# X loaded by column quarters and transposed before it is normalised, with the norm applied at the projections' outputs

## The chip, the cores and the metric

The kernel runs on one core of one Trainium2 chip. The metric is the time of one execution on the device, in microseconds (us). The kernel before takes 2932.31 us, the median of three runs (2931.34 to 2933.71).

## The reference, cut to what matters

The input is x, 256 tokens by 2048 columns, float32. Two attention layers come first (the loop over DEPTH below), then a third mixed layer, an expert layer and a final norm. The change touches the front of each of the two attention layers: the norm and the two kinds of projection by w_in.

```
def _rms_norm(x, g):
    xf = x.astype(jnp.float32)
    y = xf * lax.rsqrt(jnp.mean(xf * xf, axis=-1, keepdims=True) + NORM_EPS)
    return (y * g.astype(jnp.float32)).astype(x.dtype)

def _layer(x, g_pre, g_post, w_in, ...):
    h = _rms_norm(x, g_pre)
    proj = jnp.einsum('bsd,de->bse', h, w_in)
    (a_q, a_k, a_v, a_g, b_cq, b_ckv, b_kr, b_g, c_q, c_k, c_v, c_g) = jnp.split(proj, ...)
    ...                      # three attentions, each times silu of its gate
    y = jnp.einsum('bse,ed->bsd', jnp.concatenate([o_a, o_b, o_c], axis=-1), w_out)
    return x + _rms_norm(y, g_post)
```

The scale 1/rms is one number for each token. It can be multiplied in before the product with w_in or behind it.

## The kernel before

All matrix products are made from split operands: a float32 matrix is cut into a high part and a low part, and three products (high by high, low by high, high by low) are summed. The weights come from HBM as a stream of units of 128x2048 numbers (1 MB) into `ring`, which has four slots (R = 4); SyncE (SP) issues their loads, the next one of a slot when the slot's low part has been taken (`lo_done`). For each unit ScalarE (ACT) copies the high part to `wh` (`high`, `next_high`), VectorE (DVE) subtracts to get the low part `wl` (`low`, `next_low`), and TensorE (PE) then makes its products and adds one to `unit_done`. Four units are a group.

A layer has TM_G = 6 groups of products with tokens as rows (`rows_group`, result in PSUM, then to `PT`), FM_G = 6 groups with features as rows (`up`, result to `PF`), one group for latents, the attention in 8 rounds, and 4 groups of the output projection (`PLACE`). In this text unit n of a layer is the n-th of the first stage, counted from 0: PE makes 16 products with `wh` in it (L532) and then 8 with `wl`.

Ahead of the first group the operand is made. GpSimd (POOL) gives `rstd2`, the 1/rms of each token, from square sums that ACT makes in the first layer (`square_sums`); for the second layer POOL works it out from sums of the output projection. DVE multiplies X by it, block by block of 512 columns (`normed`, to `Xn`, `xn_done`); PE transposes `Xn` in four parts of 8 transposes (`transposed`, L601, `ht_full`); ACT takes from PSUM the high part `hh` of each chunk, with the gain `gcol` as its scale (`nh_done`), and DVE the low part `hl` (`nl_done`). Unit s of group 0 needs part s of both (`norm_part`). In the second layer X itself is first completed by `x_block`, which needs `yr` of POOL.

Beside this runs a second stream: 192 tiles of the matrix `in_ada`, loaded by POOL's queue into the two slots of `aring` and reduced by DVE (`modulation`, L1941), which belongs to the third layer and is spread over the whole program. DVE's loop over the units of the first stage is `if j > 1: next_low(...)` and then `modulation(l_ada, j)`, so the first two tiles stand ahead of the low part of unit 3, and everything on DVE runs in the order in which it is written. POOL issues the first tile behind `rstd_of(0, sq_done, prs_done)`. No scheduler moves anything; the order on each engine is that of the code, save that the compiler places the loads of ACT's function tables (ACT_TABLE_LOAD).

`keep_awake(n, bank)` makes n products of the identity with itself, of which nobody reads the result. Before, 40 of them stand at the end of each layer.

Of the kernel before, what the change touches and what calls it, by code (L numbers as in the profile page):

```python
# [23 lines left out]
P = 128  # L24
# [4 lines left out]
ALU = mybir.AluOpType  # L29
# [21 lines left out]
R = 4  # L51
# [29 lines left out]
ADA_TM, ADA_FM, ADA_ATT, ADA_WO = 22, 18, 2, 16  # L81
# [86 lines left out]
FM_MODS = [()] * 11 + [(0,), (1, 2), (3,), (4, 5), (6,), (7, 8), (9,), (10, 11), (12,), (13, 14), (15,), (16,), (17,)]  # L168
# [31 lines left out]
def block(nc, stream, ada, cond, small, const1, const2, decays, keys, nbr_bias, g_post, g_final, x, out):  # L200
# [8 lines left out]
    with ctx:  # L209
# [69 lines left out]
        krot = area(0, 2, T, 64)  # L279

# [101 lines left out]
        x_load = [sem(f"x_load{j}") for j in range(3)]  # L382
# [19 lines left out]
        yrs_done = sem("yrs_done")  # L402
        pe_passed, pool_passed, dve_passed = sem("pe_passed"), sem("pool_passed"), sem("dve_passed")
# [45 lines left out]
        def _(sp):  # L449
            sp.dma_start(ring[:, 0, :], stream[0]).then_inc(w_ready[0], 16)  # L450
            sp.dma_start(SM[:, :], small).then_inc(small_ready, 16)
            sp.dma_start(X[:, 0, :], x[0, 0:P, :]).then_inc(x_load[0], 16)
            for half in range(2):
                cols = slice(half * (DM // 2), (half + 1) * (DM // 2))
                sp.dma_start(X[:, 1, cols], x[0, P:2 * P, cols]).then_inc(x_load[1 + half], 16)
            sp.dma_start(crow, cond.rearrange("p (a b) -> p a b", a=2)).then_inc(cond_ready, 16)
            for s in range(1, R):
# [38 lines left out]
        def _(pe):  # L496
# [85 lines left out]
            def prenorm(i, banks):  # L582

                for b in range(8):
                    if b % 2 == 0:
                        pe.wait_ge(xn_done, i * 8 + (b + 2))
# [7 lines left out]
            def transposed(i, part, banks=T_BANKS):  # L594

                pe.wait_ge(xn_done, i * 8 + 2 * (part + 1))
                for b in (2 * part, 2 * part + 1):
                    for kk in range(2):
                        k = 2 * b + kk
                        for t in range(T):  # L600
                            last = pe.transpose(ps[:, banks[b], kk * SEQ + t * P:kk * SEQ + (t + 1) * P],  # L601
                                                Xn[:, t, k * P:(k + 1) * P], ident)
                    last.then_inc(ht_full, 1)

            pe.wait_ge(small_ready, 16)
            with pe.Fori(0, LAYERS) as l:
                for part in range(3):
                    transposed(l, part)
                for i in range(TM_G - 2):
                    rows_group(l * LAYER_G + i, l * TM_N + i, i % 2, layer=None if i else l, rest=() if i else ((l, 3),))  # L610
                for p, cols in ((0, 512), (1, TM_END)):
# [2466 lines left out]
```

## Time and profile before

| what | value |
|---|---|
| median of 3 runs | 2932.31 us (2931.34 to 2933.71) |
| the profiled execution | 2940.65 us, span 2939.0 us |
| PE busy | 2896.1 us, 99% of the span |
| PE weight load busy | 2480.1 us, 84% |
| DVE busy | 2127.9 us, 72% |
| ACT busy | 1309.7 us, 45% |
| POOL busy | 331.1 us, 11% |
| mean granted clock of PE | 0.995 |
| DMA | 620.62 MB, mean 211 GB/s |

The span is the time from the first to the last instruction of the profiled execution. A busy PE is not a PE at its peak, since the ends of pipelined matmuls are modelled; what the table says is that PE hardly ever waits. What can be gained or lost by an edit away from PE is thus in the few places where PE does wait.

### The profile page before, as it was taken

How to read it: one execution, taken by the hardware profiler on the slowest of the kernel's cores; microseconds unless marked ns; L12 is line 12 of the kernel's file. 1: busy time of each engine (PE TensorE's matmuls, PEld its weight loads, DVE VectorE, ACT ScalarE, POOL GpSimd, SP SyncE). 2: the span in 40 equal slices, each digit the busy share in tenths (PEclk: the TensorE clock that was granted, in tenths of full speed). 3: DMA queues.
4: the chain of work that ended last, by engine and by line, in shares of the span. 5: the costliest groups of instructions: out<-in, count | busy, mean ns of one | idle time of the engine just before them, and what ended most of it. 6: DMA issues, size and time to landing. Idle time of an engine off the chain costs nothing.

```text
span 2939.0 us, 43097 instructions
## 1 busy us (share of the span) xinstructions
PE 2896.1 (99%) x15984; PEld 2480.1 (84%) x15984; DVE 2127.9 (72%) x2852; ACT 1309.7 (45%) x1660; POOL 331.1 (11%) x359
## 2 busy tenths in 40 slices
PE   7999999999999999999999999999999999999998
PEld 6888788888788898988888888888888888887886
DVE  5687777687776857777489688447874488888745
ACT  5343444443544334754355444444443444444433
POOL 1011020011021101020088300000000000000001
PEclk9999999999999999999999999999999999999999
DMA  8867477766567867266545544555455554454553
GB/s 318 297 220 280 171 261 261 276 249 243 196 233 268 305 252 265 92 216 228 186 172 186 186 179 178 187 199 186 173 183 186 195 188 175 171 186 173 189 196 143
DMA packets 99614, 620.62 MB, mean 211 GB/s; under 512 B 11056, under 2 KB 11184, under 8 KB 37040
## 3 DMA queue, kind: packets, MB, share of 16 engines
q1 hardware_dynamic: 70560, 509.88, 48.3%
q0 software_dynamic: 28944, 109.26, 10.5%
q8 instruction: 71, 1.16, 0.2%
q14 instruction: 39, 0.32, 0.0%
HBM read 616.99 MB, written 2.10 MB: 211 GB/s over the span
## 4 chain that ended last, share of the span: by engine, by line
PE 90%; DVE 4%; DMA 3%; issue 1%; ACT 1%; POOL 1%; DVEq 0%; POOLq 0%; SPq 0%; ACTq 0%
PE ps L568 29%; PE ps L1015 17%; PE ps L532 15%; PE ps L578 15%; PE ps L1091 5%; DMA aring<-in_ada 2%; PE ps L977 1%; PE ps L741 1%; DVE wl L1925 1%; DVE aring L1941 1%; ACT BIG L1180 1%; PE ps L780 0%; PE ps L856 0%; PE ps L662 0%; PE ps L716 0%
## 5 line engine op out<-in xcount | busy, mean ns | idle before, releaser
L1180 ACT ACTIVATE wh<-ring 128x2048 fp32r<-128x2048 f32 (+1 forms) x498 | 894.6, 1802 | 1320.0 <-PE ps L578 668.3
L1925 DVE TENSOR_TENSOR wl<-ring,wh 128x2048 fp32r<-128x2048 f32 (+1 forms) x433 | 985.9, 2277 | 570.2 <-ACT wh L1180 308.6
L568 PE MATMUL ps<-hhl,wh 128*128 128x512 f32 x3680 | 889.9, 394 | 0.2 <-ACT wh L1180 0.2
L568 PEld LDWEIGHTS ps<-hhl,wh 128*128 128x128 f32 x3680 | 677.6, 189 | 132.9 <-issue 0.9
L578 PEld LDWEIGHTS ps<-hhl,wl 128*128 128x128 f32 x3680 | 471.7, 191 | 18.7 <-DVE wl L1925 0.8
L578 PE MATMUL ps<-hhl,wl 128*128 128x256 f32 x3680 | 477.1, 283 | 0.4 <-DVE wl L1925 0.4
L532 PE MATMUL ps<-wh,hhl 128*128 128x512 f32 (+1 forms) x1728 | 403.9, 386 | 2.2 <-issue 1.8
L532 PEld LDWEIGHTS ps<-wh,hhl 128*128 128x128 f32 x1728 | 320.2, 189 | 66.1 <-issue 3.7
L1941 DVE SCALAR_TENSOR_TENSOR aring<-aring,BIG 128x1024 f32<-128x1024 f32 x192 | 233.0, 1220 | 52.8 <-DMA aring<-in_ada 51.0
L532 PE MATMUL ps<-wl,hhl 128*128 128x512 f32 (+1 forms) x864 | 209.0, 384 | 1.4 <-DVE wl L1925 1.4
L1706 POOL DMA_DIRECT2D aring<-in_ada x192 | 102.3, 533 | 856.7 <-DVE aring L1941 839.0
L1015 PE MATMUL ps<-wh,stage_h 128*128 128x512 f32 x736 | 196.9, 389 | 0.0
L1015 PE MATMUL ps<-wl,stage_h 128*128 128x512 f32 x736 | 196.7, 389 | 0.0
L1015 PE MATMUL ps<-wh,stage_l 128*128 128x512 f32 x736 | 196.7, 389 | 0.0
L532 PEld LDWEIGHTS ps<-wl,hhl 128*128 128x128 f32 x864 | 159.6, 188 | 32.9 <-DVE wl L1925 2.0
L1822 POOL TENSOR_TENSOR wl<-ring,wh 128x1024 fp32r<-128x1024 f32 x62 | 152.0, 2480 | 125.9 <-ACT wh L1180 125.9
L1015 PEld LDWEIGHTS ps<-wh,stage_l 128*128 128x128 f32 x736 | 138.2, 188 | 28.7
L1015 PEld LDWEIGHTS ps<-wl,stage_h 128*128 128x128 f32 x736 | 138.2, 188 | 28.7
L1180 ACT ACTIVATE BIG<-ps 128x256 f32<-128x256 f32 (+5 forms) x171 | 100.0, 591 | 139.7 <-PE ps L532 84.9
L1015 PEld LDWEIGHTS ps<-wh,stage_h 128*128 128x128 f32 x736 | 137.9, 188 | 28.8 <-DVE stage_l L2540 0.4
L1827 POOL TENSOR_TENSOR X<-X,act 128x512 f32<-128x512 f32 x4 | 5.1, 1300 | 1275.3 <-DVE act L2886 1275.3
L1091 PE MATMUL ps<-wh,pairs 128*128 128x512 f32 x480 | 136.1, 395 | 1.7 <-DVE pairs L2755 1.7
(311 smaller groups left out, 2502.8 us busy)
## 6 DMA issues: line engine op xcount, KB each, us to landing
ring<-in_stream SPq DMA_DIRECT2D x480, 1024.0 KB, 4.8
aring<-in_ada POOLq DMA_DIRECT2D x192, 512.0 KB, 5.0
BIG<-in_nbr_bias POOLq DMA_DIRECT2D x2, 1024.0 KB, 6.2
BIG<-in_g_post POOLq DMA_DIRECT2D x2, 1024.0 KB, 5.6
out<-X SPq DMA_DIRECT2D x4, 512.0 KB, 2.7
BIG<-in_decays POOLq DMA_DIRECT2D x2, 768.0 KB, 5.9
X<-in_x SPq DMA_DIRECT2D x1, 1024.0 KB, 7.1
X<-in_x SPq DMA_DIRECT2D x2, 512.0 KB, 8.9
```

Source lines behind the costliest of these rows:

```text
L532: last = mm(ps[:, 2 * pair + t, 0:cols], lhs[:, k, tok], rhs[:, s % 2, w], start=s == 0 and kk == 0 and j == 0, stop=s == R - 1 and kk == ...
L568: mm(ps[:, 4 + c, :], wh[:, c % 2, k * P:(k + 1) * P], hhl[:, k, :, :].rearrange("p a b -> p (a b)"), start=(k == 0), stop=False, skip_gro ...
L578: last = mm(ps[:, 4 + c, 0:SEQ], wl[:, c % 2, k * P:(k + 1) * P], hh[:, k, :], start=False, stop=(k == KD - 1), skip_group_check=True)
L741: last = mm(ps[:, 6 + buf, hh2 * SEQ:(hh2 + 1) * SEQ], v, probT[buf][:, hh2, kt, :], start=(kt == 0), stop=(kt == 1))
L977: last = mm(ps[:, bank + j // 4, at:at + GATE_PARTS * PART], hot1[:, b, j, :], hot2[:, b, :, j, :], start=True, stop=True)
L1015: last = mm(ps[:, 4 * t + d, :], lhs[:, c % 2, tok], rhs[:, c % 2, d * 512:(d + 1) * 512], start=first and j == 0, stop=last_unit and j == ...
L1091: last = mm(ps[:, 4 * t + 2 * p + d, :], pairs[c % 2][:, part, i2, tok], rhs[:, c % 2, at:at + 512], start=first and i2 == 0 and j == 0, s ...
L1180: return nc.scalar.activation(o, i, func, **kw)
L1706: pool.dma_start(aring[:, h, :], ada[first + i, h]).then_inc(a_ready[h], 16)
L1822: pl.tensor_tensor(wl[:, c % 2, cols], ring[:, c, cols], wh[:, c % 2, cols].bitcast(F32), ALU.subtract).then_inc(lo_done if half else lo_h ...
L1925: return tt(blocks(wl[:, c % 2, :], cols), blocks(ring[:, c, :], cols), blocks(wh[:, c % 2, :].bitcast(F32), cols), ALU.subtract)
L1941: stt(w, w, 1.0, crow[:, h, :], ALU.mult, ALU.mult, accum_out=mod_parts[:, bass.ds(first * 2 + j, 1)]).then_inc(a_used, 1)
```

## The change

- SP loads the small constants first, then in turn a quarter of X's columns (all 256 tokens by 512 columns, `x_load[0..3]`) and a weight unit; `cond` comes after unit 2.
- PE begins with 16 identity products. It transposes X itself, not `Xn`, each part as its quarter has landed; parts 0 and 1 stand ahead of unit 0, parts 2 and 3 between units 0 and 1. In the second layer each part waits for its `x_block` alone. The loop over the two layers is written out on PE. The 40 identity products behind layer 0 become 20; behind layer 1 they stay 40.
- `normed` goes from both layers. The scale is put in later: ACT's copies of the first stage's groups become two each, one for each token tile, with scale `rstd2` (`rooted_out`); for the second stage PE makes a row of the scales in PSUM by two products (`root_row`), DVE copies it to `rrow`, and POOL multiplies each of the 24 chunks of `PF` by it (`fm_scaled`). ACT's Silu of a gate chunk now waits for this product. The table `FM_MODS` puts 16 instead of 18 tiles of `in_ada` into the second stage, and the first has 24 instead of 22.
- In the first layer ACT makes the square sums behind the high part of unit 3, no longer at the start, and the high and low parts of unit 0 come after the first two chunks of the operand.

```
             sp.dma_start(SM[:, :], small).then_inc(small_ready, 16)
+            for s in range(R):
+                cols = slice(s * 512, (s + 1) * 512)
+                sp.dma_start(X[:, :, cols], x[0, :, cols].rearrange("(t p) c -> p t c", t=T)).then_inc(x_load[s], 16)
                 sp.dma_start(ring[:, s, :], stream[s]).then_inc(w_ready[s], 16)
+                if s == 2:
+                    sp.dma_start(crow, cond.rearrange("p (a b) -> p a b", a=2)).then_inc(cond_ready, 16)
...
+            def root_row(l):
+
+                pe.wait_ge(prs_done, l + 1)
+                for t in range(T):
+                    last = mm(ps[:, 7, t * P:(t + 1) * P], rstd2[:, t:t + 1].to_broadcast([P, P]), ident, start=True, stop=True)
+                last.then_inc(rrow_full, 1)
+
             pe.wait_ge(small_ready, 16)
-            with pe.Fori(0, LAYERS) as l:
-                for part in range(3):
+            keep_awake(16, 7)
+            for l in range(LAYERS):
+                for part in range(2):
                     transposed(l, part)
                 for i in range(TM_G - 2):
-                    rows_group(l * LAYER_G + i, l * TM_N + i, i % 2, layer=None if i else l, rest=() if i else ((l, 3),))
+                    rows_group(l * LAYER_G + i, l * TM_N + i, i % 2, layer=None if i else l, rest=() if i else ((l, 2), (l, 3)))
+                root_row(l)
...
-                keep_awake(40, 7)
+                keep_awake(20, 7)
+            keep_awake(20, 7)
...
+            def rooted_out(g, col, pair, cols=512):
+                act.wait_ge(unit_done, g * R + R)
+                for t in range(T):
+                    last = f(PT[:, t, col:col + cols], ps[:, 2 * pair + t, 0:cols], ACT.Copy, scale=rstd2[:, t:t + 1])
+                last.then_inc(tm_free, 1)
...
-            high(0, 0, True).then_inc(hi_done, 1)
-            square_sums()
+            act.wait_ge(x_done, 2 * LAYERS)
             for l in range(LAYERS):
...
                 for b in range(8):
                     if b == 2 and l == 0:
+                        high(0, 0, True).then_inc(hi_done, 1)
+                    if b == 4 and l == 0:
                         next_high(l * LAYER_G, 0, True)
...
                 for c in range(2, R):
                     next_high(l * LAYER_G, c)
-                rows_out(PT, l * LAYER_G, 0, 0)
+                    if l == 0 and c == 2:
+                        square_sums()
+                act.wait_ge(prs_done, l + 1)
+                rooted_out(l * LAYER_G, 0, 0)
...
+                for j in range(FM_G * R):
+                    pool.wait_ge(fm_free, l * FM_C + j + (R + 1))
+                    pool.sem_inc(pool_passed, 1)
+                    pl.tensor_tensor(PF[:, j, :], PF[:, j, :], rrow, ALU.mult).then_inc(fm_scaled, 1)
```

What this makes of the order at three places is shown here. The first is ACT at the very start of the program; `hhl<-ps,gsc` is the high part of a chunk of the operand, `wh<-ring` that of a weight unit, `BIG,stat<-X` a square sum. Before:

```order
L1180 ACT_TABLE_LOAD
L1180 ACTIVATE wh<-ring 128x2048 [waits w_ready0]
L1180 ACTIVATE BIG,stat<-X 128x2048 [waits x_load0]
L1180 ACTIVATE BIG,stat<-X 128x1024 [waits x_load1]
L1180 ACTIVATE BIG,stat<-X 128x1024 [waits x_load2]
L1180 ACTIVATE hhl<-ps,gsc 128x256 [waits ht_full]
```

And of the change:

```order
L1196 ACT_TABLE_LOAD [waits ht_full]
L1196 ACTIVATE hhl<-ps,gsc 128x256 [waits x_done]
L1196 ACTIVATE hhl<-ps,gsc 128x256
L1196 ACTIVATE hhl<-ps,gsc 128x256 [waits ht_full]
L1196 ACTIVATE hhl<-ps,gsc 128x256
L1196 ACTIVATE wh<-ring 128x2048 [waits w_ready0]
```

The square sums have left the start, unit 0's high part has moved behind two chunks of the operand, and the table load now carries the wait for the first transposes.

The second place is ACT further on, behind the last chunk of the operand of the first layer, in the change. Before, these rows stood in the same order without the three of `BIG,stat<-X`:

```order
L1196 ACT_TABLE_LOAD
L1196 ACTIVATE BIG<-BIG 128x2048 [waits cond_ready]
L1196 ACTIVATE wh<-ring 128x2048 [waits unit_done,w_ready3]
L1196 ACTIVATE BIG,stat<-X 128x2048 [waits x_load2,x_load3,x_load1,x_load0]
L1196 ACTIVATE BIG,stat<-X 128x1024 x2
L1196 ACTIVATE wh<-ring 128x2048 [waits unit_done,w_ready0]
L1196 ACTIVATE BIG<-ps,stat 128x512 [waits unit_done,prs_done]
```

The square sums now stand between the high parts of units 3 and 4, and the scaled copy of group 0 waits for what POOL makes of them.

The third is DVE and POOL. On DVE the rows behind the last low part of the operand, in the change (before, they are the same, but the first has `c1_ready` in place of the four `x_load`):

```order
L2043 SCALAR_TENSOR_TENSOR hhl<-ps,gsc,hhl 128x256
L1990 SCALAR_TENSOR_TENSOR aring,mod_parts<-aring,BIG 128x1024 [waits nl_done,x_load2,x_load3,x_load1,a_ready0,x_load0,c_ready]
L1990 SCALAR_TENSOR_TENSOR aring,mod_parts<-aring,BIG 128x1024 [waits a_ready1]
L1974 TENSOR_TENSOR wl<-ring,wh 128x2048 [waits hi_done]
L1990 SCALAR_TENSOR_TENSOR aring,mod_parts<-aring,BIG 128x1024 [waits a_ready0]
```

And on POOL, from the start, in the change (before, the same, with three `x_load`):

```order
L1752 DMA BIG<-in_const 128x1536 [waits x_load2,x_load1,x_load3,x_load0,small_ready]
L1723 ISA [waits sq_done]
L1723 TENSOR_TENSOR stat<-stat 128x1
L1716 TENSOR_SCALAR stat<-stat 128x2 [waits pool_step]
L1718 TENSOR_TENSOR stat<-stat,SM 128x2 [waits pool_step]
L1754 TENSOR_SCALAR stat<-stat 128x2
L1736 UNCONDITIONAL_BRANCH
L1736 ISA
L1741 ISA [waits a_used]
L1741 DMA aring<-in_ada 128x1024
```

On DVE nothing moved: the `wl<-ring,wh` there is the low part of unit 3, behind two reductions of `aring`. On POOL the issue of `aring`'s first load still follows the wait for `sq_done`, and it is `sq_done` that has moved, on ACT.

## Rows read from the trace of the kernel before

**Rows 1.** The page: busy time of each engine, share of the span, instructions.

```profile
PE 2896.1 (99%) x15984; PEld 2480.1 (84%) x15984; DVE 2127.9 (72%) x2852; ACT 1309.7 (45%) x1660; POOL 331.1 (11%) x359
```

**Rows 2.** Timeline, 0 to 45 us: start, duration, engine, line, tiles, count, idle before.

```profile
1.32 0.42 SPq L451 DMA_DIRECT2D SM<-in_small  x1
...
8.91 1.91 ACT L1180 ACTIVATE BIG<-X 128x2048 f32<-128x2048 f32 x1 [1.17 <-DMA X<-in_x]
...
13.11 0.19 ACT L1180 ACTIVATION_READ_ACCUMULATOR BIG<-X 128x1 f32 x1
...
15.27 1.37 POOL L1706 DMA_DIRECT2D aring<-in_ada  x2
...
16.19 5.29 PE L601 MATMUL ps<-SM,BIG 128*128 128x128 f32 x24 [16.19 <-DVE BIG L1854]
17.34 1.69 ACT L1180 ACTIVATE hhl<-ps,gsc 128x256 fp32r<-128x256 f32 x4 [4.04 <-PE ps L601]
...
21.22 3.91 PE L532 MATMUL ps<-wh,hhl 128*128 128x512 f32 x16
...
30.44 1.28 ACT L1180 ACT_TABLE_LOAD   x1
...
31.74 1.92 ACT L1180 ACTIVATE BIG<-BIG 128x2048 f32<-128x2048 f32 x1
...
33.69 1.23 DVE L1941 SCALAR_TENSOR_TENSOR aring<-aring,BIG 128x1024 f32<-128x1024 f32 x1 [0.81 <-ACT BIG L1180]
...
35.98 2.28 DVE L1925 TENSOR_TENSOR wl<-ring,wh 128x2048 fp32r<-128x2048 f32 x1
...
38.59 3.79 PE L532 MATMUL ps<-wh,hhl 128*128 128x512 f32 x16
...
44.03 3.79 PE L532 MATMUL ps<-wh,hhl 128*128 128x512 f32 x16
```

**Rows 3.** DMA issues (KB, us to landing), and a window of 2 us with its GB/s last.

```profile
SM<-in_small SPq DMA_DIRECT2D x1, 230.5 KB, 5.1
```

```profile
3.00:5.00 2.00, 0.00 (x0) 0.00 (x0) 0.00 (x0) 0.00 (x0) 0.00 (x0) 1.00 1.02 430
```

**Rows 4.** Timeline, 430 to 462 us: from the first layer to the second.

```profile
430.39 9.09 PE L509 MATMUL ps<-SM 128*128 128x128 f32 x80
...
434.29 2.74 DVE L1860 SCALAR_TENSOR_TENSOR X<-BIG,stat,X 128x512 f32<-128x512 f32 x4 [1.01 <-POOL stat L1762]
...
441.21 2.83 PE L601 MATMUL ps<-SM,BIG 128*128 128x128 f32 x24 [1.73 <-DVE BIG L1854]
...
444.69 3.92 PE L532 MATMUL ps<-wh,hhl 128*128 128x512 f32 x16 [0.64 <-issue]
...
456.92 3.79 PE L532 MATMUL ps<-wh,hhl 128*128 128x512 f32 x16
...
458.55 0.53 POOL L1706 DMA_DIRECT2D aring<-in_ada  x1 [18.32 <-DVE aring L1941]
...
461.94 1.23 DVE L1941 SCALAR_TENSOR_TENSOR aring<-aring,BIG 128x1024 f32<-128x1024 f32 x1 [0.50 <-DMA aring<-in_ada]
```

**Rows 5.** Windows: length, busy PE, PEld, DVE, ACT, POOL, granted clock, DMA share, GB/s.

```profile
439.48:441.21 1.73, 0.00 (x0) 0.00 (x1) 1.73 (x5) 0.00 (x0) 0.63 (x2) 1.00 0.53 152
865.43:866.83 1.40, 0.00 (x1) 0.00 (x0) 0.66 (x3) 1.37 (x3) 0.00 (x0) 1.00 0.00 0
867.90:874.70 6.80, 6.80 (x22) 5.70 (x22) 6.73 (x11) 2.66 (x2) 1.09 (x3) 0.51 0.01 2
...
1372.50:1376.70 4.20, 4.20 (x12) 3.29 (x13) 3.83 (x6) 4.14 (x7) 0.00 (x0) 0.59 0.00 0
```

**Rows 6.** The page's row of POOL's subtraction; timeline of the second stage.

```profile
L1822 POOL TENSOR_TENSOR wl<-ring,wh 128x1024 fp32r<-128x1024 f32 x62 | 152.0, 2480 | 125.9 <-ACT wh L1180 125.9
```

```profile
211.12 0.41 DVE L1934 TENSOR_TENSOR BIG<-BIG,ps 128x256 f32<-128x256 f32 x1
...
214.29 0.42 ACT L1180 ACTIVATE BIG<-BIG 128x256 f32<-128x256 f32 x1
```

More of the change, by code:

```diff
@@ L592, in prenorm, with transposed @@
                     last.then_inc(ht_full, 1)
[L594 to L596 removed]
+            def transposed(i, part, banks=T_BANKS, src=X):
+                if i:
+                    pe.wait_ge(xn_done, (i - 1) * 8 + 2 * (part + 1))
+                else:
+                    pe.wait_ge(x_load[part], 16)
                 for b in (2 * part, 2 * part + 1):
@@ L1182, in square_sums @@
             def square_sums():
-                act.wait_ge(x_load[0], 16)
+                for part in range(4):
+                    act.wait_ge(x_load[part], 16)
                 f(Xn[:, 0, :], X[:, 0, :], ACT.Square, accum_out=ss2[:, 0:1]).then_inc(sq_done, 1)
                 for half in range(2):
-                    act.wait_ge(x_load[1 + half], 16)
                     cols = slice(half * (DM // 2), (half + 1) * (DM // 2))
@@ L1233, in next_high, with rooted_slots @@
                 high(g + (c + 1) // R, (c + 1) % R, free, cols).then_inc(hi_done, 1)
+            def rooted_slots(g, col, pair, cols=512, after=512):
+                for c in range(R):
+                    next_high(g, c, False, cols if c < R - 1 else after)
+                rooted_out(g, col, pair, cols)
+            def rooted_out(g, col, pair, cols=512):
[3 more added lines that the diff above has]
+                last.then_inc(tm_free, 1)
             def rows_slots(dst, g, col, pair, free=False, cols=512, after=512):
@@ L1284, in _ @@
                     if 2 <= j < GATE_CHUNKS + 2:
-                        shape(PF, l * FM_C + (j - 2), j - 2, ACT.Silu)
+                        shape(PF, l * FM_C + (j - 2), j - 2, ACT.Silu, fm_scaled)
                 for j in (FM_C - 2, FM_C - 1):
@@ L1969, in rotate @@
                 return tt(dst, dst, tmp, ALU.add)
-            low(0, 0).then_inc(lo_done, 1)
             dve.wait_ge(small_ready, 16)
-            for j in range(3):
-                dve.wait_ge(x_load[j], 16)
             dve.sem_inc(tm_free, 2)
@@ L1993, in _ @@
             take_gains(0)
+            dve.sem_inc(x_done, 2 * LAYERS)
             for l in range(LAYERS):
-                dve.wait_ge(prs_done, l + 1)
-                for block in range(3):
-                    if l:
-                        if block == 2:
-                            x_block(l - 1, block)
-                        next_block(l - 1, block)
-                    else:
-                        normed(block)
                 for b in range(8):
@@ L2009, in _ @@
                     ins.then_inc(nl_done, 1)
+                    if l and b in (1, 3):
+                        x_block(l - 1, 2 + b // 2)
+                    if b == 1 and l == 0:
+                        low(0, 0).then_inc(lo_done, 1)
                     if b == 3:
                         next_low(l * LAYER_G, 0)
-                        if l:
-                            x_block(l - 1, 3)
-                            next_block(l - 1, 3)
-                        else:
-                            normed(3)
                     elif b == 5:
@@ L2022, in _ @@
                 dve.wait_ge(c_ready, 1)
-                dve.wait_ge(c1_ready, 16)
+                for part in range(4):
+                    dve.wait_ge(x_load[part], 16)
                 l_ada = l * (ADA_LAYER // 2)
```

73 lines of the change are left out of this document (42 added, 31 removed).

## The prediction, made before the change was run

> **What bounds the kernel now.** I read the page first. PE is busy for 99% of the span, DVE for 72%, ACT for 45% [rows 1], and the chain of work that ended last runs over PE's matmuls nearly everywhere. So an edit on another engine is worth what it takes from, or adds to, the places where PE waits. The timeline shows two of them in the stretch that the change touches. At the start PE does nothing until 16.19 us; 24 transposes follow, and unit 0 begins at 21.22 [rows 2]. Units 3 and 4 begin at 38.59 and 44.03, which is 5.44 us for a unit; from there on PE's units follow each other without a gap. At the passage to the second layer PE makes its 40 identity products from 430.39 (9.09 us), idles 1.73 us, transposes from 441.21, begins unit 0 at 444.69 and unit 2 at 456.92 [rows 4]. I take the start of unit 4 in the first layer and of unit 2 in the second as the two points at which to compare, because behind them the supply is ahead of PE.
>
> **The start, step by step.** The small constants were issued second, behind 1024 KB, and landed 5.1 us after their issue at 1.32 [rows 2, 3], so at 6.4; without the 1024 KB ahead, at the 430 GB/s of that stretch [rows 3], they land 2.45 us sooner, at 4.0. PE then makes 16 identity products. The 40 of before are 80 records in 9.09 us [rows 4], so each counts as two, and 16 are 32 records. They take 0.114 us each at full speed, and about 0.22 at the start: the 24 transposes there took 5.29 us, where the same 24 took 2.83 us at 441.21 [rows 2, 4]. PE reached full speed after 5.0 us of work (16.19 to 21.22). So I count 23 records at 0.22 and 9 at 0.114, 6.0 us, to 10.1. The first two quarters of X have landed by then: 230 KB, 512, 1024 and 512 at 430 GB/s end at 9.0. Four transposes (0.44) and the hop to ACT of 0.27 (16.19 plus 0.88 to 17.34) give 10.8.
>
> Here ACT's table load stands with its wait for the transposes, where before it was done while nothing was there to do. It costs 1.28 us [rows 2]: 12.1. Four copies of the operand (1.69): 13.8. High part of unit 0 (1.9, as the copy of its shape at 31.74): 15.7, and PE starts unit 0 at 15.8, 5.4 us sooner than before. PE had ended its second part of transposes at 11.9, so it idles 3.9 us ahead of it.
>
> Unit 0 to 21.4, 16 transposes (1.75, of which before had 8 here) to 23.1, unit 1 to 28.6, units 2 and 3 behind it. But unit 3 needs its low part, and that is behind two reductions of `aring` on DVE, which need loads that POOL issues behind `sq_done`. Before, the squares were over at 13.30 and the issue at 15.27 [rows 2], and nobody waited. Now the squares are on ACT behind the high part of unit 3. ACT from 22.1 (0.7 behind the end of unit 0): four copies 1.7, the high part of unit 2 1.9, four copies 1.6, to 27.3; table load and Silu 3.2 (30.44 to 33.66), to 30.5; high part of unit 3, 1.9, to 32.4; squares 4.4 (8.91 to 13.30), to 36.8. POOL to its issue 2.0 (13.30 to 15.27): 38.8. The load, into an idle queue, 3.4: the nearest rows are the issue at 458.55 and DVE's take at 461.94 [rows 4]. That is 42.2. Two reductions 2.4 (33.69 to 35.98, and a hop): 44.6; low part of unit 3, 2.3: 46.9; its 8 products 1.8. So unit 4 starts at **48.8 instead of 44.03: +4.8 us**. PE stands still in unit 3 from about 37.8 to 46.9, 9 us. Who waits: PE for DVE, DVE for the DMA, POOL for ACT. Behind it the second pair of tiles is reloaded while unit 3's low part is made, so low parts 4 and 5 come before PE needs them.
>
> **The clock.** The granted clock was 0.51 for 6.8 us from 867.9, after PE had idled 1.40 us and then made narrow products, and 0.59 for 4.2 us from 1372.5; it was 1.00 in the 1.73 us of idleness at 439.48 and after it [rows 5]. One such dip costs 6.8 x 0.49 = 3.3 us or 4.2 x 0.41 = 1.7 us, and the ramp at the start 5.0 / 2 = 2.5 us. I take 2.7. After 9 us of idleness in unit 3 I count one in full; the bounds are 0 and 3.3. Before unit 0, 3.9 us of idleness is over twice what went without a dip, so I count one there too, 2.7 us: unit 0's end feeds ACT's chain above, so it goes through to unit 4. The start is then +4.8 +2.7 +2.7 = **+10.2 us**.
>
> **The passage to the second layer.** The first two blocks of X are done two at a time from 434.29 by 0.685 us each [rows 4]: 435.7 and 437.0. PE transposes from 435.8, and the second part to 438.0. What goes is the wait for `rstd2`, `normed` and the backward jump of PE's loop, all between 437.0 and the transposes at 441.21. ACT's first two pairs of copies end at 438.1, DVE's low parts at 439.1, and unit 0 starts at 439.2 instead of 444.69. It takes 5.5, then 16 transposes 1.8 (8 before), unit 1 5.5: unit 2 starts at 452.0 instead of 456.92, **-4.9 us**. DVE makes blocks 2 and 3 of X (1.4 each) between low parts, by 443.5, ahead of PE's need at 444.7. The idle stretches of PE here: 20 identity products are 4.55 us, to 434.7, then 1.1, 0.4 and 1.2 us, none as long as the 1.73 without a dip. I count no dip; the bound is 3.3.
>
> The Trainium skill (TensorE: Matmul & The Clock Gate, the section on HAM oscillation) says that the engine falls back to half its clock when it has been left idle long enough, and that every such gap is paid again. By that rule alone the two long gaps of the start are cold and the short ones of the passage are not; a sum that left it out would be +4.8 for the start and end near no change. The dip at 867.9 followed only 1.40 us of full idleness, so the row is harsher than the rule.
>
> **The small parts.** `root_row` is two float32 products, four records, 0.46 us a layer on PE: **+0.9 us** for both. ACT's 12 copies cut in two cost some 0.2 us each and hide in ACT's 45% load. POOL's product of 128x256 is a quarter of the 128x1024 of 2.48 us, 0.62 us [rows 6]; the column sum of a chunk ended at 211.53 and ACT's Silu took it at 214.29, 2.8 us later [rows 6], so it fits in. If it did not, ACT would be late, and PE only beyond another 2.5 us or so. Two more tiles in the first stage: DVE has about 2 us a unit to spare. The gone `normed` was hidden except at the passage. All at nothing, bound +1.
>
> **Sum:** +10.2 - 4.9 + 0.9 = **+6.2 us**. The terms come from an execution of 2940.65 us (span 2939.0, 1.65 around it), 8.3 us above the median; what it adds is spread over the program, so the sum goes onto the median: 2932.3 + 6.2 = **2938.5 us**.
>
> **Rivals.** A measurement of this kernel tells about 0.2%, 5.9 us, from no change, and the sum lies just beyond it.
> (a) Forecast: stall in unit 3, both dips: +6.2, 2938.5. With a dip also at the passage +9. Chance 0.50 for all that comes beyond +5.9.
> (b) The stall with one dip or none at the start: +3.5 or +0.8, 2935.8 or 2933.1, and ACT's chain 1 us quicker or slower. For it: the record of a dip is irregular, as the idleness at 439 shows. 0.42. It becomes (a) where the dips together cost over 5.1 us.
> (c) Faster. One mechanism: the first two tiles land before DVE comes to them, because the square sums find ACT free earlier. Then PE keeps the lead of unit 1, 28.6 against 33.15, and the start is -4.5 (-1.8 with the dip before unit 0), the passage -4.9: -8.5, 2923.8. It decides from the point where `sq_done` comes before 26.3 us, 10.5 sooner than I have it. Against it: the order of the rows on ACT, which puts the squares behind a high part that itself waits for unit 1. 0.08, with what I have not seen.
> (d) POOL becomes the bound of the second stage: its 24 products each held up as long as 5.3 us more. Then shape, ACT and PE slow down by some 0.5 us a unit, +24 us for two layers. POOL has 5.57 us a unit and is needed for 0.62. 0.02, within (a)'s chance.
> Range: leaving out (c) and the far end, from one dip fewer and a chain 2 us quicker (2931.5) to three dips at 3.3 and a chain 2 us slower (2945.5). Slower 0.50, same 0.42, faster 0.08.
>
> **What would show it.** Right: unit 0 at about 15.8, a PE gap of about 9 us that ends with a low part of DVE, behind it `aring`'s load issued at about 39; unit 4 at 49 to 54; a clock below 1 behind the gap; the second layer's unit 0 some 5 us closer to its `x_block`. Wrong: a table load done at 0.9 us (then 1.3 us less), identity products at full speed (2 us less), no gap in unit 3, Silu in the second stage waiting for POOL.

## The result and the profile after

The changed kernel takes 2939.4 us, the median of 22 runs (2936.43 to 2944.76); the kernel before, run beside it, 2934.79 us (22 runs, 2931.33 to 2939.58). The ratio is 1.0014, 95% interval [1.0009, 1.0020]: slower by about 4 us, within the 0.2% that I called no change. The profiled execution has a span of 2936.6 us against 2939.0 before, so a single pair of profiles ranks the two the wrong way round, and the stages have to be compared one by one.

The timeline of the start, as those of [rows 2] (start, duration, engine, line, tiles, count, idle before):

```profile
3.50 6.12 PE L509 MATMUL ps<-SM 128*128 128x128 f32 x32 [3.50 <-DMA SM<-in_small]
...
9.46 1.04 PE L604 MATMUL ps<-SM,X 128*128 128x128 f32 x8
10.14 1.28 ACT L1196 ACT_TABLE_LOAD   x1 [10.14 <-PE ps L604]
10.89 1.09 PE L604 MATMUL ps<-SM,X 128*128 128x128 f32 x8 [0.40 <-DMA X<-in_x]
11.44 1.57 ACT L1196 ACTIVATE hhl<-ps,gsc 128x256 fp32r<-128x256 f32 x4
...
14.86 5.52 PE L532 MATMUL ps<-wh,hhl 128*128 128x512 f32 x16 [2.87 <-ACT wh L1196]
...
22.04 1.91 PE L604 MATMUL ps<-SM,X 128*128 128x128 f32 x16
...
32.44 1.90 ACT L1196 ACTIVATE BIG<-X 128x2048 f32<-128x2048 f32 x1
...
36.32 0.19 ACT L1196 ACTIVATION_READ_ACCUMULATOR BIG<-X 128x1 f32 x1
...
38.35 1.30 POOL L1741 DMA_DIRECT2D aring<-in_ada  x2
42.19 1.22 DVE L1990 SCALAR_TENSOR_TENSOR aring<-aring,BIG 128x1024 f32<-128x1024 f32 x1 [12.24 <-DMA aring<-in_ada]
...
44.52 2.29 DVE L1974 TENSOR_TENSOR wl<-ring,wh 128x2048 fp32r<-128x2048 f32 x1
...
46.86 3.78 PE L532 MATMUL ps<-wl,hhl 128*128 128x512 f32 x8 [8.36 <-DVE wl L1974]
...
50.44 4.86 PE L532 MATMUL ps<-wh,hhl 128*128 128x512 f32 x16
```

Read it from the end backwards. The low products of unit 3 waited 8.36 us for DVE. DVE had been idle 12.24 us until its first `aring` tile landed, which POOL had asked for at 38.35, when ACT's square sums (32.44 to 36.51) were done. All of this gap is new. The clock in the stretch behind the gap (columns as in [rows 5]):

```profile
42.70:52.70 10.00, 5.84 (x14) 4.59 (x15) 8.68 (x10) 1.96 (x3) 1.58 (x3) 0.50 0.68 230
```

It is at its lower level, 1.2 GHz, and products that take 1.98 and 3.79 us elsewhere take 3.78 and 4.86. At unit 0 the order is another: the clock is still at 1.00 through the 2.87 us of idleness, and falls within the products.

```profile
14.00:15.00 1.00, 0.14 (x1) 0.14 (x2) 0.16 (x1) 1.00 (x2) 0.00 (x0) 1.00 1.00 418
...
16.00:17.00 1.00, 1.00 (x4) 0.72 (x3) 1.00 (x1) 1.00 (x2) 0.00 (x0) 0.50 0.98 410
```

Unit 5 starts at 56.95 instead of 49.47, 7.5 us later. The passage, as in [rows 4]:

```profile
438.19 4.63 PE L509 MATMUL ps<-SM 128*128 128x128 f32 x40
...
442.09 2.74 DVE L1909 SCALAR_TENSOR_TENSOR X<-BIG,stat,X 128x512 f32<-128x512 f32 x4 [1.01 <-POOL stat L1811]
...
443.56 1.09 PE L604 MATMUL ps<-SM,X 128*128 128x128 f32 x8 [0.74 <-DVE X L1909]
444.88 1.09 PE L604 MATMUL ps<-SM,X 128*128 128x128 f32 x8 [0.23 <-DVE X L1909]
446.89 3.88 PE L532 MATMUL ps<-wh,hhl 128*128 128x512 f32 x16 [0.91 <-issue]
...
452.43 1.91 PE L604 MATMUL ps<-SM,X 128*128 128x128 f32 x16
...
459.66 3.79 PE L532 MATMUL ps<-wh,hhl 128*128 128x512 f32 x16
```

From the first identity product to unit 2 it is 21.47 us, before 26.53 [rows 4]: 5.06 us less, with no wait for a root or for `Xn` and no slow product. And the second stage, where POOL has its new product (L1776), in a stretch of four instructions and in the groups of 140 to 290 us (count, busy, mean ns, idle before and its cause):

```profile
222.29 1.22 DVE L1990 SCALAR_TENSOR_TENSOR aring<-aring,BIG 128x1024 f32<-128x1024 f32 x1
222.55 1.55 POOL L1776 TENSOR_TENSOR BIG<-BIG 128x256 f32<-128x256 f32 x1 [4.18 <-DVE BIG L1983]
...
223.43 2.82 DVE L1974 TENSOR_TENSOR wl<-ring,wh 128x2048 fp32r<-128x2048 f32 x1
...
224.22 0.42 ACT L1196 ACTIVATE BIG<-BIG 128x256 f32<-128x256 f32 x1 [1.86 <-POOL BIG L1776]
```

```profile
L1974 DVE TENSOR_TENSOR wl<-ring,wh 128x2048 fp32r<-128x2048 f32 x24 | 57.7, 2405 | 6.5 <-ACT wh L1196 6.4
...
L1776 POOL TENSOR_TENSOR BIG<-BIG 128x256 f32<-128x256 f32 x24 | 33.8, 1407 | 67.0 <-DVE BIG L1983 61.8 <-issue 5.2
...
L1776 POOL TENSOR_TENSOR BIG<-BIG x24: 717/1546/1827, 163.7 to 287.9; 128x256 f32<-128x256 f32 x24
140.00:290.00 150.00, 150.00 (x890) 134.47 (x889) 123.66 (x133) 65.70 (x74) 50.52 (x49) 1.00 0.74 269
```

(The line with three numbers has the shortest, median and longest of the 24 products, in ns.) The product takes 1.4 us in the mean, from 0.72 to 1.83, and DVE's low part, 2.29 us by itself, takes 2.82 beside it; but PE is busy for 150.00 of 150 us, so none of it shows in this stretch.

### The profile page after: what moved, and what is told of

Read it like the earlier page. It is cut to its first block, busy times and chain, and to the rows that moved or that the text cites. A ratio compares the mean times of both kernels' runs of the same rounds, so it can differ in the third digit from the quotient of the medians.

```text
span 2936.6 us, 42937 instructions
## 1 busy us (share of the span) xinstructions
PE 2897.6 (99%) x15984; PEld 2480.4 (84%) x15984; DVE 2134.7 (73%) x2838; ACT 1313.8 (45%) x1672; POOL 399.3 (14%) x407
## 4 chain that ended last, share of the span: by engine, by line
PE 95%; DVE 2%; ACT 1%; POOL 1%; issue 1%; DMA 0%; DVEq 0%; POOLq 0%; ACTq 0%
PE ps L568 29%; PE ps L532 19%; PE ps L1031 17%; PE ps L578 15%; PE ps L1107 5%; PE ps L993 1%; PE ps L756 1%; ACT BIG L1196 1%; PE ps L796 0%; PE ps L872 0%; PE ps L676 0%; PE ps L730 0%; DVE BIG L2432 0%; PE ps L1092 0%; PE ps L1059 0%
## 5 line engine op out<-in xcount | busy, mean ns | idle before, releaser
L1741 POOL DMA_DIRECT2D aring<-in_ada x156 | 82.8, 531 | 672.4 <-DVE aring L1990 660.8
L1196 ACT ACTIVATE BIG<-ps 128x256 f32<-128x256 f32 (+5 forms) x159 | 88.1, 560 | 102.9 <-PE ps L532 47.6
```

The costliest lines, as they stand in the source:

```text
L1196: return nc.scalar.activation(o, i, func, **kw)
L1741: pool.dma_start(aring[:, h, :], ada[first + i, h]).then_inc(a_ready[h], 16)
```

## The experiments

All are edits of the changed kernel. Each was timed beside the kernel before on its chip (28 to 32 runs of it, medians 2934.73 to 2935.79), and the ratio is to that one. It is a ratio over all the runs and not the quotient of the two medians: with the gap filled the medians alone would give 0.9961, but two of that version's nine runs took 2930 and 2935 us. The recorded expectations call two tiles first e1, and a unit n of the start un.

| version | median us | ratio [95%] | unit 4, unit 6 start | end of layer 0 |
|---|---|---|---|---|
| before | 2934.79 | 1 | 44.03, 54.91 | 430.39 |
| changed | 2939.4 | 1.0014 [1.0009, 1.0020] | 50.44, 62.39 | 438.19 |
| two tiles first | 2929.25 | 0.9978 [0.9970, 0.9987] | 40.28, 52.98 | 429.92 |
| two tiles, table | 2935.22 | 0.9997 [0.9988, 1.0005] | 38.96, 57.64 | 433.81 |
| waits at the passage | 2942.39 | 1.0025 [1.0016, 1.0034] | 50.91, 61.82 | 438.68 |
| POOL's product twice | 2958.1 | 1.0071 [1.0058, 1.0084] | 50.16, 61.77 | 445.44 |
| four tiles first | 2927.48 | 0.9974 [0.9965, 0.9984] | 40.00, 50.88 | 427.64 |
| four tiles, table | 2928.28 | 0.9979 [0.9969, 0.9989] | 39.54, 50.42 | 426.22 |
| no identity at the passage | 2939.67 | 1.0017 [1.0008, 1.0026] | 50.76, 62.13 | |
| POOL's product on one column | 2940.15 | 1.0017 [1.0008, 1.0025] | 50.58, 62.60 | 440.05 |
| four tiles, none in front | 2927.97 | 0.9973 [0.9964, 0.9981] | 38.33, 49.21 | 425.03 |
| four tiles, gap filled | 2924.45 | 0.9972 [0.9961, 0.9982] | 38.98, 49.86 | 425.64 |
| four tiles, table, lows first | 2930.84 | 0.9982 [0.9973, 0.9991] | 38.46, 51.99 | 431.54 |
| all | 2928.92 | 0.9981 [0.9973, 0.9990] | 37.59, 50.02 | 427.19 |

The last columns are from the one profiled execution of each: the first product with `wh` of units 4 and 6, and the first identity product behind layer 0.

**Two tiles first.** My theory of the start was that the gap is an order of three queues: PE waits for DVE, DVE for a tile, POOL asks for the tile behind the square sums. The rival: the tiles matter little, and PE is late because ACT is.

```
             for j in range(4):
                 pool.wait_ge(x_load[j], 16)
+            tile(0)
+            tile(1)
             pool.dma_start(area(C1, CONST1_W), const1).then_inc(c1_ready, 16)
             rstd_of(0, sq_done, prs_done)
...
-                modulation(l * (ADA_LAYER // 2), ADA_TM)
+                modulation(l * (ADA_LAYER // 2) + (l == 0), ADA_TM - 2 * (l == 0))
```

> The changed kernel, with POOL issuing the first two tiles of in_ada before it waits for the square sums. Theory (the late square sums hold back the tiles, the tiles hold back the low part of unit 3): the gap of 8.4 us in unit 3 goes, and with it the dip of the clock behind it. The high part of unit 4 is ready at about 38.4, so unit 4 starts at about 40.2 instead of 50.2 and unit 5 at 45.6 instead of 57.0, and the kernel takes 11 us less than the changed kernel, 7 less than before (ratio 0.9976). Rival (the stall is set by ACT, which carries the square sums ahead of unit 4's high part, or by the DMA traffic at the start): a gap of several us stays, only moved to unit 4, and the kernel gains less than 5 us.

```profile
38.49 1.30 POOL L1741 DMA_DIRECT2D aring<-in_ada  x2
...
42.07 1.23 DVE L1992 SCALAR_TENSOR_TENSOR aring<-aring,BIG 128x1024 f32<-128x1024 f32 x1 [6.59 <-DMA aring<-in_ada]
...
45.57 2.12 PE L532 MATMUL ps<-wl,hhl 128*128 128x512 f32 x8 [1.50 <-DVE wl L1976]
```

Confirmed: unit 3 has no gap, the slow clock behind it is gone too, and the time falls 0.36% below the changed kernel and 0.22% below the one before. What is left is a gap of 1.50 us in unit 4: the third and fourth tile are still asked for behind the square sums.

**The table load brought forward.** The same with a copy of one column on ACT in front, which takes the table load out of the wait for the first transposes.

```
+            act.wait_ge(small_ready, 16)
+            f(stat[:, 383:384], one, ACT.Copy)
             act.wait_ge(x_done, 2 * LAYERS)
```

> As e1_tiles_first, and ACT makes one copy of one column as soon as the small constants are there, so that its table load is done before the first transposes. Theory (the table load stands in the chain to unit 0): unit 0 starts 1.3 us earlier than in e1, at about 13.6, and so does unit 5; time 1.3 us below e1, more if the dip at unit 0 goes with the shorter idleness, and less if the last quarter of X (21.3) then holds unit 1. Rival (unit 0 waits for its weights or for X): no change against e1.

```profile
44.19 1.22 DVE L1994 SCALAR_TENSOR_TENSOR aring<-aring,BIG 128x1024 f32<-128x1024 f32 x1 [7.24 <-DMA aring<-in_ada]
```

```profile
47.68 3.78 PE L532 MATMUL ps<-wl,hhl 128*128 128x512 f32 x8 [4.92 <-DVE wl L1978]
```

A miss by the time. The first units did gain (unit 0 at 13.81 and in 3.96 us), and unit 4 started 1.3 us sooner, but the third tile, asked for at 37.98, was there only at 44.19, 6.2 us later (3.6 in the version before it). PE waited 4.92 us and the clock fell again. The square sums were done 2.7 us earlier than with two tiles alone (33.91 against 36.65), and the request came only 0.5 us earlier. The reason is in two rows:

```profile
34.66 2.29 DVE L1978 TENSOR_TENSOR wl<-ring,wh 128x2048 fp32r<-128x2048 f32 x1
...
35.00 2.00 POOL L1718 TENSOR_SCALAR stat<-stat 128x2 f32<-128x2 f32 x1 [0.21 <-POOL stat L1725]
```

POOL's step of two columns on the way to the root, 0.19 us in the changed kernel, took 2.00 us beside DVE's low part and ended with it. The earlier start had brought the two together.

**The passage.** With the old wait and the old 40 identity products behind layer 0:

```
                 if i:
+                    if i == 1 and part == 0:
+                        pe.wait_ge(prs_done, 2)
                     pe.wait_ge(xn_done, (i - 1) * 8 + 2 * (part + 1))
...
-                keep_awake(20, 7)
-            keep_awake(20, 7)
+                keep_awake(40, 7)
```

> The changed kernel, with one part of its passage to the second layer undone: the first transposes of layer 1 wait for rstd2 (prs_done) as they did before, and the 40 identity products behind layer 0 are back. Everything else stays. Theory (the passage gains because nothing waits for POOL's chain any more): the transposes start at the end of the 40 products, about 3.6 us later against the output projection's end, the span from that end to unit 2 grows by 3.5 us, and the kernel takes 3.5 us more than the changed one (ratio to before about 1.0027). Rival (the gain came from the loop written out on PE alone, not from the removed wait): no change within 1 us.

Confirmed: 1.0025, and from the first identity product to unit 2 it is 25.00 us (438.68 to 463.68) instead of 21.47. So 3.5 of the 5.06 us are the wait and the products that filled it. The other 1.5 are two parts: from the first identity product to the first transposes this version still takes 1.9 us less than the one before (8.93 against 10.82 us), where `normed` is gone, and from there to unit 2 it takes 0.4 more.

**POOL's product twice.** The first of the two goes to a spare area.

```
+                    steps(pl.tensor_tensor(spare[:, 0:SEQ], PF[:, j, :], rrow, ALU.mult))
+                    steps.done()
                     pl.tensor_tensor(PF[:, j, :], PF[:, j, :], rrow, ALU.mult).then_inc(fm_scaled, 1)
```

> The changed kernel, with POOL's product of each of the 24 chunks made twice (the first time into a scratch area, and waited for), so some 1.6 us more of POOL for each. Theory (POOL's products are hidden behind PE): PE's units of the second stage stay at 5.57 us each and the time is that of the changed kernel within 1 us, though ACT's Silu waits longer. Rival (POOL is already near the bound of that stage, since its product takes 1.55 us and not the 0.62 of the prediction): Silu and then the next high part come late, PE gaps appear in the second stage, and the kernel takes 5 to 20 us more.

```profile
L1778 POOL TENSOR_TENSOR BIG<-BIG 128x256 f32<-128x256 f32 x22 | 34.2, 1552 | 1.7
L1776 POOL TENSOR_TENSOR spare<-BIG 128x256 f32<-128x256 f32 x22 | 27.3, 1239 | 45.5 <-DVE BIG L1985 40.1 <-issue 5.2
```

```profile
L578 PE MATMUL ps<-hhl,wl 128*128 128x256 f32 x379 | 49.7, 284 | 3.3 <-DVE wl L1976 3.3
```

My theory fell: the time grew by about 17 us (1.0071 against 1.0014). ACT now waits for POOL up to 5.3 us a chunk, is late with the next `wh`, DVE with `wl`, and PE shows gaps of 0.4 to 0.9 us at five chunks (3.3 us in these 150) and one of 3.1 us at 295.6. The changed kernel's product is hidden, but with a cover of less than one more product, not with the 5 us a unit that I had given it.

**POOL's product on one column.** The counterpart: the wait stays, the work goes. The gate part is left without its norm.

```
-                    pl.tensor_tensor(PF[:, j, :], PF[:, j, :], rrow, ALU.mult).then_inc(fm_scaled, 1)
+                    pl.tensor_tensor(PF[:, j, 0:1], PF[:, j, 0:1], rrow[:, 0:1], ALU.mult).then_inc(fm_scaled, 1)
```

> The changed kernel, but POOL's product of every PF chunk with the row of roots is made for one column of 256 only, so the gate part is left without its norm (that part of the computation is left out); waits and signals stay. Theory: the product is hidden in the changed kernel although it takes 1.4 to 1.8 us and not 0.62 (TensorE is busy in all of 140 to 290 and 480 to 860 us), so the time stays within 1 us of the changed kernel, ratio 1.0014, and DVE's operations beside it are back at 2.29 us. Rival: the products beside it cost 2 to 5 us through the lengthened DVE operations, that is they are the reason for all of the loss; then the ratio is 1.0000 or lower.

```profile
L1974 DVE TENSOR_TENSOR wl<-ring,wh 128x2048 fp32r<-128x2048 f32 x24 | 55.1, 2294 | 19.1 <-ACT wh L1196 18.9
...
L1776 POOL TENSOR_TENSOR BIG<-BIG 128x1 f32<-128x1 f32 x24 | 18.5, 770 | 81.4 <-DVE BIG L1983 76.9 <-issue 4.4
```

Confirmed: the time does not move, and DVE's low part is back at 2.29 us. A product of a single column still has 0.77 us in the mean, from 0.18 to 1.27. The shortest, 0.18 for one column and 0.72 for 256, are those begun when DVE has hardly any work on two operands left; the long ones are begun beside it. So the product itself is some 0.7 us, near the 0.62 that I had scaled, and the rest of its mean of 1.41 is waiting for DVE.

**Four tiles first.** Now POOL asks for the third and fourth tile too before the root:

```
             tile(0)
-            tile(1)
+            for n in range(1, 4):
+                tile(n)
```

> The changed kernel with the order of the experiment that asks for two tiles first, and in it the third and fourth modulation tile too are asked for ahead of const1 and of the root of the means. Theory: what is left of the start's loss is that these two stand in POOL's queue behind the sums of squares (asked for at 38.49 there, used from 42.07, and the low products of unit 4 wait 1.50 us). They would now be asked for at about 32.1 and 33.3, when DVE has used the first two, and DVE can make the fourth low part by about 39: no gap in unit 4, and 1.5 us less than the two tiles alone: ratio about 0.9973 of before, some 2927.7 us. Rival 1, the transfers: the tiles would then take their place among the weights' transfers and the gap moves to a weight; the ratio stays at 0.9978. Rival 2, the root comes later because POOL waits for DVE before it: then the first group's sums come out later than the products of group 1 need the banks, and the time is 1 to 3 us longer than with two tiles.

The trace shows the gap in unit 4 gone and unit 6 at 50.88 instead of 52.98; the ratio is 0.9974 where the theory gave 0.9973, though its interval also holds the 0.9978 of two tiles, so the time alone does not confirm it. **With the table load forward:**

> The four tiles asked for first, and besides the one-column copy on ACT that brings the table load ahead of its wait. Theory: the table load is worth 1.3 us, and the slow first high products of unit 0 some 1.5 us more (u0 came at 13.81 and took 3.96 us in the version with two tiles, against 14.99 and 5.51); there, what was won was lost again to the third and fourth tile (a gap of 4.92 us and a slow clock in unit 4). With these two asked for early the gain stays: 2 to 2.5 us below the four tiles alone, ratio about 0.9965. Rival: the early start only brings the compute forward against the transfers (X's quarters, the tiles and the first weights come as they come), and DVE or PE waits for a tile or for a weight in units 3 to 5; then the ratio is that of the four tiles alone, or worse by a fall of the clock, 0.9973 to 0.999.

```profile
30.50 1.22 DVE L1995 SCALAR_TENSOR_TENSOR aring<-aring,BIG 128x1024 f32<-128x1024 f32 x1 [2.67 <-DMA aring<-in_ada]
...
34.10 1.23 DVE L1995 SCALAR_TENSOR_TENSOR aring<-aring,BIG 128x1024 f32<-128x1024 f32 x1 [2.37 <-DMA aring<-in_ada]
```

```profile
37.59 2.11 PE L532 MATMUL ps<-wl,hhl 128*128 128x512 f32 x8 [1.24 <-DVE wl L1979]
```

The rival was right: the tiles, asked for at 21.5 among X, `cond` and the weights at some 420 GB/s, land 9 and 12.6 us later, and the 2 us won at unit 0 are 0.46 at unit 4. The theory's 0.9965 lies outside the interval. **Low parts ahead of the tiles** on DVE, so that none waits for a tile:

```
-                    if j > 1:
+                    if l and j > 1:
                         next_low(l * LAYER_G + j // R, j % R)
+                    if l == 0 and j + 2 < (TM_G - 2) * R:
+                        next_low((j + 2) // R, (j + 2) % R)
                     modulation(l_ada, j)
```

> The version with four tiles and the early table load, in which, for the first layer, DVE makes the low part of unit j+3 before the product with modulation tile j instead of that of unit j+1. Theory: there the low products of unit 3 waited 1.24 us for DVE, which waited for tile 0 (until 30.50) and tile 1 (until 34.10) before it made them; with the low part first it is ready at about 33, nothing waits for a tile, and the 1.24 us come back: u5 at about 43.7 instead of 44.98, ratio 0.9966 to 0.9972 (from 0.9979 measured, or 0.9970 by its trace). Rival: DVE now waits for a free wl buffer before it takes the tiles, the tiles are asked for later, and the gap comes back in unit 4 or 5: no gain.

```profile
40.70 0.53 POOL L1749 DMA_DIRECT2D aring<-in_ada  x1 [5.16 <-DVE aring L1995]
...
43.26 0.18 POOL L1759 TENSOR_SCALAR stat<-stat 128x2 f32<-128x2 f32 x1
```

```profile
46.41 3.93 PE L532 MATMUL ps<-wh,hhl 128*128 128x512 f32 x16 [2.35 <-ACT wh L1196]
```

The rival's result (a gap in unit 5), its path longer than it named: DVE takes the second tile later, so POOL asks for the fourth at 40.70 and is done with the root only behind it (at 43.26); ACT's scaled copies of group 0 wait for the root, the high part of unit 5 stands behind them, and PE waits 2.35 us for it.

**The identity products at the start.** Four tiles, without the 16 in front; and four tiles with 10 more in the gap ahead of unit 0:

```
-            keep_awake(16, 7)
...
                 for part in range(2):
                     transposed(l, part)
+                if l == 0:
+                    keep_awake(10, 0)
```

> The four-tiles version without the 16 identity products that stand before the first transposes. In it X's first quarter had landed at 1.3 + 5.4 = 6.7, the products in front ended at about 9.3, and only then came the transposes, ACT's table load (9.99) and the first high products (14.70, at 5.53 us, clock 0.5). Theory: the products in front cost more than they give, since the clock falls before unit 0 all the same: the transposes would start at 6.8, the table load at about 7.8, unit 0 at about 12.7, and with all of unit 0 in the slow clock (7.6 at the most) the stage still is 0 to 2 us earlier: ratio about 0.9970. Rival: from a standstill the clock is low for longer, unit 0's low products too are slow, and the time is that of the four tiles or 1 to 2 us more, ratio 0.9974 to 0.998.

> The four-tiles version with 10 identity products more between the first transposes and unit 0 (into a bank that unit 0 overwrites), where TensorE stood still for 2.80 us. Theory: the fall of the clock at unit 0 comes from this standstill; 20 rows of 114 ns fill 2.3 us of it, the high products of unit 0 take 3.9 instead of 5.53 us, and the start is 1.6 us earlier; as the tiles come no earlier, a wait of up to 1 us for them may show in unit 3: ratio 0.9969 to 0.9973. Rival: the clock falls there whatever stands in the gap, or the tiles' landing eats all: 0.9974.

Without the 16 in front:

```profile
6.53 1.94 PE L604 MATMUL ps<-SM,X 128*128 128x128 f32 x8 [6.53 <-DMA X<-in_x]
10.87 1.97 PE L604 MATMUL ps<-SM,X 128*128 128x128 f32 x8 [2.40 <-DMA X<-in_x]
12.49 5.70 PE L532 MATMUL ps<-wh,hhl 128*128 128x512 f32 x16
```

With 10 more in the gap:

```profile
11.62 2.40 PE L509 MATMUL ps<-SM 128*128 128x128 f32 x20
...
15.28 3.96 PE L532 MATMUL ps<-wh,hhl 128*128 128x512 f32 x16 [1.25 <-ACT wh L1198]
```

Both theories hold in the trace. X's first quarter had been there at 6.5 while PE was still at its identity products, which held up transposes, table load and unit 0 by 2 us; and with the gap filled the high products of unit 0 take 3.96 us at the full clock instead of 5.5. Against the four tiles alone unit 4 starts 1.7 and 1.0 us sooner. In time neither can be told from the four tiles alone by its interval, though the filled one has the lowest median of all, 2924.45 us.

**All together,** with 10 identity products in front and 5 in the gap:

> All together: four tiles first, early table load, low parts ahead of the tiles in the first layer, 10 instead of 16 identity products in front, and 5 between the first transposes and unit 0. Theory: the first transposes start at about 7 instead of 8.6, unit 0 at 12.5 or a little earlier, its high products take 3.9 us: u5 at about 42 and a ratio of 0.996 to 0.9967. Rival: unit 0 waits for X's second quarter (landed at 10.5) and for ACT's high part, which come no earlier; then it is 0 to 0.5 us below the version without these two edits.

In the trace neither: unit 0 starts at 12.11 and takes 3.89 us as the theory has it, but the root is again late behind the fourth tile, and PE waits 1.25 us in unit 5. By the time the rival holds: 0.9981 against the 0.9982 of the version without these two edits, though unit 6 starts 2 us sooner.

Part of what the start wins is lost later in the first layer. There the profile of the changed kernel has no gap in PE's work, and these have some, all for a low part of DVE: 0.9 us at 148 with two tiles first, 0.7 at 146 with four, 2.9 us in three gaps from 117 to 145 with the lows first, 0.8 in two with all. Why DVE is late there was not tested.

**No identity products behind layer 0:**

```
-                keep_awake(20, 7)
-            keep_awake(20, 7)
+                if l:
+                    keep_awake(40, 7)
```

> The changed kernel without the 20 identity products that stand behind layer 0 (40 rows, 4.63 us at 438.19), the 40 behind layer 1 as before. Theory: with no products TensorE stands still from about 437.5 until the first transposes at 443.56, the granted clock falls to about 0.5 and stays there for the transposes and the first products of the second layer; unit 0 takes 5.5 instead of 3.9 us, the transposes some 1 us more: 2 to 3 us longer than the changed kernel, ratio about 1.0023. Rival: the transposes and root rows keep the clock up as they come, no fall; the ratio stays at 1.0014.

```profile
443.53 3.67 PE L604 MATMUL ps<-SM,X 128*128 128x128 f32 x16 [5.21 <-DVE X L1909]
447.38 4.05 PE L532 MATMUL ps<-wh,hhl 128*128 128x512 f32 x16 [0.18 <-issue]
```

```profile
444.00:446.00 2.00, 2.00 (x11) 2.00 (x11) 1.25 (x4) 1.31 (x4) 1.59 (x6) 0.50 0.00 0
```

A miss in size by the trace. After 5.21 us of idleness the clock is at half, as expected, but that falls on the transposes, whose time was partly idleness anyway, and it is back at 2.4 GHz just behind the start of unit 0. Counted from the first `x_block`, the 20 products are worth 0.5 us at unit 0 and 0.7 at unit 2. The time decides nothing: its interval holds the theory's 1.0023 and the rival's 1.0014.

## Why the prediction was right, and where it was not

Predicted 2938.5, measured 2939.4; the sum was +6.2, the medians differ by 4.6, the ratio says 4.1. The nearness is partly luck: my base, the median of three runs, lies 2.5 us below that of all 22, and the sum was 1.6 to 2.1 us too high. By my own boundary of 5.9 us the outcome is "same", to which I gave 0.42, and not "slower", to which I gave 0.50.

**The stall** was the main term and right in place, cause and order: asked for at 38.35 (38.8 predicted), landed 42.19 (42.2), low part ready for PE at 46.86 (46.9). The table load stood behind the first transposes with its 1.28 us. Two tiles asked for earlier removed the stall, and the time fell by 10 us.

**The term that was mis-sized is the dip before unit 0.** I had added its 2.7 us on top of those times, so that the sum had the low part at 49.6 and not at 46.9. It cost 1.6 (5.52 us against the 3.91 of before), and unit 0 began at 14.86, not 15.8, so that PE ended it 2.1 us sooner than the sum with its dip had. ACT then needed 14.5 us from there to the end of the squares, where I had 15.4. The start came to +7.5, not +10.2. The gap before unit 0 was 2.9 us, not 3.9. With the gap filled the clock stayed up, so the dip hangs on what PE does there; that the length of the gap decides it is not shown, since 1.11 us went with a dip and 2.03 without. The two dips came to 1.6 + 2.9 = 4.5 us, less than the 5.1 at which I let rival (b) turn into (a): the mechanism was that of (a), the size that of (b).

**X's quarters** were taken to land one after the other. The second, counted at 9.0, landed at 10.9, and the last only at 21.3. It cost nothing here, as ACT was at its table load, but it is why POOL asked for no tile before about 21 us in any of the experiments.

**The dip behind the stall** was counted at 2.7 and measured 2.9: 3.78 and 4.86 us against 1.98 and 3.79.

**The passage** was -4.9 and measured -5.06, without a dip, as counted.

**The root rows** were +0.46 a layer and measured +0.3 in both: the end of layer 0 is 7.8 us later where unit 5 was 7.5.

**POOL's product at nothing** was right for the time and wrong in its reason. I took 0.62 us, a free engine and 2.8 us of cover. The profile has 1.4 us, and ACT waiting 1.7 to 1.9 us for it at times, which is one of the signs that I had named as wrong; a second such product, 1.4 us more for each chunk, costs 17 us. Rival (d) was much nearer than its 0.02. In the rows above POOL's product, begun at 222.55, ended 0.67 us behind the end of DVE's reduction (223.43), and DVE's low part, begun then, took the 0.53 us more. One begun at 163.69 took 1.83 us and ended 0.68 behind the end of such a DVE instruction, one begun at 169.33 took 0.75 and ended 0.67 behind it; what DVE ran next to this last one was a reduction with one operand. Both instructions read two operands from SBUF. The Trainium skill (SBUF — State Buffer, the section Who interferes with whom) has the rule: a DVE instruction with two SBUF inputs and a GpSimd instruction that reads SBUF exclude each other, and the second waits for the first. The trace agrees with it in the rows just given, and so do the one-column products with their 0.18 to 1.27 us; the prediction should have weighed it.

**The sum in the trace** is then +7.5 - 5.1 + 0.7 = +3.1 us, and it is there: the first transposes behind layer 1 start at 866.54 against 863.46. The 1 to 1.5 us between that and the medians I can't place. Short falls of the clock later in the program differ from one profile to the next. The first unit behind layer 1 has high products of 6.30 us instead of 3.92 in the profile of before, 5.50 in the changed kernel, 3.92 with two or four tiles first, but 6.41 with none in front and 6.27 with the lows first. Products that take 9.11 us at 1372.50 before take 7.97 in the changed kernel. This is more than the difference sought. It goes some way to show why the single profile of before is the longer one, and what decides it stays open.

**Rival (c)**, faster, had the state that the experiments then made, tiles that land before DVE comes to them, though it had it from earlier square sums and not from earlier requests. It gave 8.5 us less than before; the best ratio, 0.9972, is 8.2 less. That is no test of (c) in the changed kernel, where the tiles came late.

## What to carry to other kernels

When work is moved later on one engine, look at what other queues wait for its signal and what stands behind that wait in each: here square sums cost nothing themselves, and everything that POOL would issue behind them cost 10 us. A request for data belongs ahead of waits that it does not need. But each request that itself waits (here for a free slot of `aring`) holds back what stands behind it, as the fourth tile held back the root. Behind an early start, check the next arrival: 2 us won at unit 0 came to 0.5 at unit 4, as the transfers came when they came.

## What the runs showed of the hardware

- A float32 product on POOL: 0.72 us for 128x256 and 0.18 for 128x1 at the shortest, 1.83 and 1.27 at the longest, beside DVE instructions with two operands in SBUF; and DVE's 2.29 us become 2.82 beside it. A step of two columns on POOL took 2.00 us instead of 0.19.
- The granted clock fell to 0.50 within unit 0's high products after 2.87, 1.97 and 1.11 us of idleness (5.52, 5.54 and 5.54 us), yet not after 2.03 in another version (3.96 us); with identity products up to 1.25 us before it, not either. So the length of the gap alone did not decide it.
- The granted clock in the rows does not show the slow start of the program: the changed kernel made 6 or 7 products of 128 columns in a microsecond from 4 to 8 us, and 11 from 9 to 10, with 1.00 in all these rows.
- The table load, 1.28 us, stands with the wait of the first instruction that needs it; a copy of one column ahead of that wait takes it off the path (it is then over before X lands).
- The same request for a tile of 512 KB took 3.6 us to land in one version and 6.2 in another, both asked for at about 38 us; no run shows why.
